# Attention on one core: one row-score pair at every key step, and the narrow sixth pair of each half job moved between the second and third value products

## What is computed

```python
def gqa_block_attention(q, k, v):           # 16 query heads, 4 key/value heads, head width 64
    ...
    def one_block(q_blk):
        s = jnp.einsum('bqhgd,bkhd->bhgqk', q_blk, k, preferred_element_type=F32) * scale
        pr = jax.nn.softmax(s, axis=-1).astype(v.dtype)
        return jnp.einsum('bhgqk,bkhd->bqhgd', pr, v)
```

## Time and profile before

| what | value |
|---|---|
| median of 3 runs | 3097.41 us (3095.95 to 3100.65) |
| span of the profiled execution | 3093.3 us |
| difference of the two (launch and end, outside the span) | 4.1 us |
| PE busy | 94% of the span |
| row scores ahead of job 0 | 807.9 to 831.58 us |
| jobs 0 to 13 and first half of job 14, with row scores | 831.58 to 1289.20 us |
| rest of the attention, without row scores | 1289.20 to 1336.40 us |
| one job in the steady part | 31.36 us |

### The profile page before, as it was taken

How to read it: one execution, slowest core, us unless ns; L and a number is a source line. 1 busy time by engine, 2 the same in 40 slices (tenths; PEclk the granted TensorE clock), 3 DMA queues, 4 the chain that set the end, 5 groups by cost and what they waited for, 6 DMA issues and landing times. The chain is left out here.

```text
span 3093.3 us, 28722 instructions
## 1 busy us (share of the span) xinstructions
PE 2916.4 (94%) x10163; PEld 1457.1 (47%) x10163; DVE 1591.3 (51%) x2480; ACT 740.7 (24%) x1557; POOL 1076.2 (35%) x971
## 2 busy tenths in 40 slices
PE   7998999999899999999969994988999999999999
PEld 4554554444455555444544442566444444444443
DVE  2433884345666666555654434446543444444446
ACT  2223755411133333300211115222030000000002
POOL 0002871000176767710022002832023445555442
PEclk9998999999899999999969996999999999999999
DMA  7001332100100000020178987003020111111101
GB/s 276 21 0 41 90 96 72 54 28 1 55 1 1 1 1 1 1 66 11 68 259 320 358 352 239 22 0 123 0 82 27 41 41 49 66 49 41 41 14 61
DMA packets 130686, 237.51 MB, mean 77 GB/s; under 512 B 25544, under 2 KB 81520, under 8 KB 120688
## 3 DMA queue, kind: packets, MB, share of 16 engines
q1 hardware_dynamic: 120016, 206.11, 18.8%
q0 software_dynamic: 5760, 16.78, 1.8%
q10 hardware_dynamic: 4768, 12.79, 1.1%
HBM read 235.65 MB, written 26.22 MB: 85 GB/s over the span
## 5 line engine op out<-in xcount | busy, mean ns | idle before, releaser
L3597 DVE TENSOR_TENSOR arena_d<-arena_d,ps 128x512 f32<-128x512 f32 x154 | 101.8, 684 | 389.2 <-PE ps L3472 389.2
L1366 DVE TENSOR_REDUCE arena_b<-ps 128x1 f32<-128x512 f32 (+1 forms) x384 | 217.3, 599 | 146.5 <-PE ps L1254 146.0
L3437 POOL TENSOR_TENSOR arena_b<-arena_b,arena_d 128x512 f32<-128x512 f32 x120 | 150.8, 1271 | 362.7 <-DVE arena_d L3619 361.3
L1348 POOL TENSOR_TENSOR arena_b<-arena_b 128x512 f32<-128x512 f32 x182 | 224.6, 1268 | 94.5 <-ACT arena_b L1330 94.5
L1254 PE MATMUL ps<-arena_d,arena_a 64*128 64x512 f32 (+1 forms) x768 | 237.1, 541 | 3.6 <-DVE arena_b L1357 2.9
L1273 PE MATMUL ps<-arena_a,arena_d 64*128 64x512 f32 x640 | 220.0, 607 | 2.4 <-ACT arena_b L1330 1.8
L3616 DVE TENSOR_TENSOR arena_b<-arena_b,ps 128x512 f32<-128x512 f32 x240 | 159.0, 685 | 32.7 <-POOL arena_b L3437 23.7
L1077 PE MATMUL ps<-ring,arena_b 128*128 128x512 f32 x384 | 167.4, 592 | 0.0
L564 PE MATMUL ps<-arena_b,ring 128*128 128x512 f32 x384 | 167.1, 593 | 0.0
L1330 ACT ACTIVATE arena_b<-ps 128x512 f32<-128x512 f32 x214 | 116.1, 595 | 212.8 <-PE ps L1279 212.8
L3472 PE MATMUL ps<-arena_a,ring 128*128 128x512 f32 x352 | 156.0, 602 | 3.0 <-DMA ring<-in_w_up 3.0
(11 more groups left out here) (614 smaller groups left out, 5492.3 us busy)
## 6 DMA issues: line engine op xcount, KB each, us to landing
ring<-in_w_gate SPq DMA_DIRECT2D x33, 1024.0 KB
ring<-in_w_up SPq DMA_DIRECT2D x33, 1024.0 KB
ring<-in_w_down SPq DMA_DIRECT2D x33, 1024.0 KB
ring<-in_w_in SPq DMA_DIRECT2D x10, 2048.0 KB, 9.8
ring<-in_w_mod SPq DMA_DIRECT2D x32, 512.0 KB, 3.8
yslots<-arena_a ACTq DMA_DIRECT2D x24, 512.0 KB, 4.5
arena_d<-in_w_gate SPq DMA_DIRECT2D x10, 1024.0 KB
arena_d<-in_w_up SPq DMA_DIRECT2D x10, 1024.0 KB
```

The costliest lines, as they stand in the source:

```text
L1348: eng.tensor_tensor(acc, first, prT[n % NPR], ALU.add).then_inc(s_pa, 1)
L1366: eng.tensor_reduce(mx3[j % 2][:, t, e, piece:piece + 1], ps[:, shared("s", u), 0:k1 - k0], AX.X, ALU.max).then_inc(s_mx, 1)
L3437: eng.tensor_tensor(o, o, dsum[0 if a == "a12" else 1], ALU.add).then_inc(s_comb, 1)
```

## The change

One row-score pair now stands at each key step: 6, 7, 8, 9, 10 in steps 0 to 4, and 0, 1, 2, 3, 4 in steps 5 to 9. The sixth pair, the narrow 11 or 5, no longer has a step. PE makes it after two of the five value products (`PV_FIRST = 2`). The order in which the three shared banks are given out follows PE's order, so in step 9 the narrow pair now takes its banks after the turned shifts and the row sums. DVE's program is changed to the same order: in step 9 it takes the maxima of the narrow pair after the copy of the shifts and ahead of the reciprocal.

```diff
-        BESIDE = (((1, 6),), ((1, 7),), ((1, 8), (1, 9)), ((1, 10),), ((1, 11),),
-                  ((2, 0),), ((2, 1),), ((2, 2), (2, 3)), ((2, 4),), ((2, 5),))
+        BESIDE = tuple((a, p) for a, p0 in ((1, 6), (2, 0)) for p in range(p0, p0 + 5))
 
         GROUP = 5
+        BETWEEN = {GROUP - 1: (1, 11), NT - 1: (2, 5)}
+        PV_FIRST = 2
...
             for j in range(NJOB):
                 for kt in range(NT):
                     shifted(j, kt)
-                    for ahead, pair in BESIDE[kt]:
-                        if j + ahead < NJOB:
-                            scores(j + ahead, pair)
+                    ahead, pair = BESIDE[kt]
+                    if j + ahead < NJOB:
+                        scores(j + ahead, pair)
                     if kt == NT - 1 and j + 1 < NJOB:
                         turn_shifts(j + 1)
                     if kt == NT - 1 and j >= 1:
                         row_sums(j - 1)
-                    if kt % GROUP == GROUP - 1:
-                        for i in range(kt + 1 - GROUP, kt + 1):
-                            pv(j, i)
+                    if kt in BETWEEN:
+                        for i in range(GROUP):
+                            if i == PV_FIRST:
+                                ahead, pair = BETWEEN[kt]
+                                if j + ahead < NJOB:
+                                    scores(j + ahead, pair)
+                            pv(j, kt + 1 - GROUP + i)
...
                 for kt in range(NT):
-                    for ahead, pair in BESIDE[kt]:
+                    ahead, pair = BESIDE[kt]
+                    if j + ahead < NJOB:
+                        largest(j + ahead, pair)
+                    if kt == NT - 1 and j + 1 < NJOB:
+                        shifts(j + 1)
+                    if kt in BETWEEN:
+                        ahead, pair = BETWEEN[kt]
                         if j + ahead < NJOB:
                             largest(j + ahead, pair)
                     if kt == GROUP - 1 and j + 1 < NJOB:
                         split(j + 1)
-                    if kt == NT - 1 and j + 1 < NJOB:
-                        shifts(j + 1)
                     if kt == NT - 1 and j >= 1:
                         scale(j - 1)
```

More of the change, by code:

```diff
@@ L1228, in build @@
             for kt in range(NT):
-                for ahead, pair in BESIDE[kt]:
-                    if j + ahead < NJOB:
-                        takes_pair(j + ahead, pair)
+                ahead, pair = BESIDE[kt]
+                if j + ahead < NJOB:
+                    takes_pair(j + ahead, pair)
                 if kt == NT - 1 and j + 1 < NJOB:
```

## The result

| | median | lowest to highest | runs |
|---|---|---|---|
| before | 3095.80 us | 3089.69 to 3100.65 | 12 |
| after | 3104.86 us | 3096.59 to 3108.19 | 12 |

A forecast was written before the change was run, and what follows sets the result against it. PE was taken as the bound, by how densely it streams. Net changeover cost of 2.6 us and 7.0 for the reciprocal sum to 9.6, making the median 3107.0 us from 3097.41, slower by 0.31%; range 3098.5 to 3112.

The forecast's parts named there:

- The double step: Third step of a half job, with two row-score pairs: weights wait for maxima, one array half lags; costs 0.78 us.
- The 9.70 of the prediction: Summed lengths of a half job's products in us, set against the 10.65 it takes, so about 0.95 is lost.
- the three places: Where a half job loses time: entry 0.10, third step 0.78, exit 0.10, together 0.98 us.
- The lag behind a lone narrow pair: Step after the third: e = 1 waits for its exponential, 0.52 us with late weights, leaving a gain of 0.26.
- Changing over: Narrow pair inside the value products: two more changes between 128-row and 64-row products cost 0.35 us a half job.
- Net +0.09 a half job: Cost 0.35 of the moved narrow pair less the 0.26 gained by spreading; x 29 = +2.6 us.
- The reciprocal: First row scores of jobs 2 to 14 wait for it behind the narrow maxima: 0.54 us, 13 times, +7.0 us.
- The offset: Profiled span 3093.3 lies 4.1 us under the median of the runs, 3097.41; the same was added to the forecast span.
- A: Rival at the next job's first row scores: the reciprocal is in time, only 2.6 us stays, 3100.0; chance 0.13.
- B: Rival at the step after the lone narrow pair: no lag, whole 0.78 gained, 3091.9 us, faster; chance 0.09.
- D: Rival at the value products: switching between 128-row and 64-row products costs nothing, 3096.8 us, no change; chance 0.04.
- C: Rival on DVE: one more long operation makes `split` end 0.3 late, 5 to 18 us more, 3112 to 3125; chance 0.07.

The follow-up runs named there:

- Experiment 5: Kernel before, with pairs dealt narrow, four full, narrow, the first ahead of the first step and one at each step: 3076.23 us, ratio 0.9940.
- experiment 4: Changed kernel with the four full pairs in steps one to four, narrow ones in the fifth step and the value products: 3088.84 us, ratio 0.9983.
- experiment 6: Kernel before, with a full pair ahead of the first step and a lone narrow pair at the second: 3088.24 us, ratio 0.9974 to the kernel before.
- Experiment 7: Changed kernel with full pairs first and DVE's reciprocal ahead of the narrow maxima: 3085.18 us, ratio 0.9972 to the kernel before.
- experiment 1: Changed kernel, but DVE takes the reciprocal and its multiplication ahead of the narrow pair's maxima: 3099.54 us, ratio 1.0016 to the kernel before.
- experiment 2: Changed kernel with the narrow pair after the first value product in place of the second: 3099.19 us, ratio 1.0015 to the kernel before.
- experiment 3: Changed kernel with the narrow pair after the third value product in place of the second: 3115.52 us, ratio 1.0068 to the kernel before.

## Why the prediction was right, step by step

**The losses of before.** The double step, 0.78 a half job, was read from rows alone. Experiment 5 shows it: with all six pairs in the half job and no double step it takes 9.95 for 10.65. These 0.70 are the 0.78 less the 0.09 of lag that every full step leaves, and that the longer lag of the double step had covered. The 9.70 of the prediction is a sum of rounded lengths; with 0.859 for a pair and 0.216 for a bf16 pair, the products of a half job stream for 9.67, and the three places, 0.98, then make up the whole 10.65.

**The lag behind a lone narrow pair.** Forecast: 10.65 - 0.43 - 0.26 = 9.96. Measured 9.95. Experiments 4 and 6 show the cause, once by taking the narrow pair from the third step and once by bringing a lone one back. The part that a mended order gets back is 0.43 and not the 0.52 of the prediction, because 0.09 of lag stands already behind every full step (the load at 1009.01 in the earlier trace rows, released by ACT, is such a one); the prediction's 0.52 was the whole, and the right number for its sum.

**Changing over.** Forecast 0.35 a half job. The value products with the pair take 5.23 for 4.44, that is 0.79, of which 0.43 is the pair: 0.36. Experiment 7 against 5 gives 0.35 again. Net +0.09 a half job and 2.6 us stand.

**The reciprocal.** The right mechanism, mis-sized: 0.54 a time was forecast, 0.37 measured, 4.8 us in place of 7.0. With T = 1022.37, the first transpose, the reciprocal ended at T + 7.90 (forecast T + 7.98), and the row scores were due at T + 7.69 (forecast T + 7.59), so the difference of the two long sums was 0.27 with the late load and not 0.44. The term that was mis-sized is the two narrow maxima. The prediction took 0.81 from the earlier trace rows and 0.03 behind them; from the start of the first (1026.25) to the start of the reciprocal (1026.92) it was 0.67. In the earlier trace rows the second maximum had waited for a lagging e = 1, and the recorded length of a maximum reaches beyond the start of the next operation: 1026.25 + 0.75 is 1027.00. All else in the two sums came 0.10 later than forecast on both sides. Experiments 1, 2 and 3 show that it is the reciprocal: it goes when DVE comes to it sooner by either way, and grows by 0.86 for 0.86.

**What was missing.** Transposes and row sums take 1.30 in place of 1.23, and the value products behind them 5.21 in place of 4.39 + 0.78 = 5.17. The fifth step now ends in a full pair, and the row sums take the bank of its e = 0. Their weights load at 1022.76, where 1022.70 would be the pace of before. Together 0.11 a job, 1.4 us over 13 jobs. The 0.07 is the wait of experiment 4 again, shorter. The maximum of e = 0 and the load of the row sums, in the changed kernel and then in experiment 4:

```profile
1021.96 0.69 DVE L1375 TENSOR_REDUCE arena_b<-ps 128x1 f32<-128x512 f32 x1 [0.65 <-PE ps L1259]
1022.76 0.23 PEld L1302 LDWEIGHTS ps<-arena_b,ones 128*64 128x64 f32 x4 [0.17 <-issue]
...
1012.24 0.42 DVE L1377 TENSOR_REDUCE arena_b<-ps 128x1 f32<-128x256 f32 x1 [0.22 <-PE ps L1260]
1012.78 0.23 PEld L1303 LDWEIGHTS ps<-arena_b,ones 128*64 128x64 f32 x4 [0.33 <-issue]
```

In both, the load comes 0.11 to 0.12 us after the end of the maximum, though one stands 0.39 behind the first transpose and the other 0.55. It is so in the steady jobs of all kernels but the kernel before and experiment 6, where the maximum is done 0.18 ahead and the load stands at 0.33. Why the value products behind them take 0.04 more, no row says.

The sum of what was measured is 29 x 0.09 + 13 x 0.37 + 1.4 = 8.8 us, against 8.9 in the attention of the trace and 8.7 by the ratio.

**The offset.** The prediction set the profiled span 4.1 us under the median. In every run of the changed kernel the time is 2.1 us over its span, so only 2.1 of the 4.1 is launch and end. The rest is that the execution profiled before was faster than the median of the three. As an offset added to before and after alike it changed nothing in the forecast difference; the median before came out at 3095.80 over twelve runs, 1.6 below the 3097.41 from which the forecast of 3107.0 was counted.

**The rivals.** A (the reciprocal in time) was close: 0.27 us decided it, and experiment 1 is that case, with 1.0016. B (no lag) and D (changing over is free) fell by the rows. C (`split` too late) did not come; it went the other way, below.

## What to carry to other kernels

When two halves of the array run beside each other, one late bank lets one half lag, and the lag (0.43 us in experiments 4 and 6) is paid at the next product that needs both. It shows in no idle time of PE, so count the streaming time of a stretch and compare. A short piece of work at a step gives the next step less time than product, exponential and weight load need behind each other (1.06 us here behind a full and behind a narrow pair alike), so short pieces belong last, or where nothing waits behind them. Spreading work evenly by number (one pair per step) isn't yet spreading it evenly by time, and a piece put into a gap elsewhere has its own price at both ends and its place in another engine's queue.

## What the runs showed of the hardware that was not expected

`split` became shorter, without any edit to it. In the earlier trace rows it takes 3.30 us from 1003.12. Two of its six operations, on 8 elements a partition, take 1.23 and 1.18 us; here they are, with two of POOL's additions from POOL's timeline:

```profile
1003.33 1.23 DVE L1376 CAST arena_b<-arena_b 128x8 bf16<-128x8 f32 x1
1004.59 1.18 DVE L1377 TENSOR_TENSOR arena_b<-arena_b 128x8 f32<-128x8 f32 x1
...
1003.23 1.29 POOL L1348 TENSOR_TENSOR arena_b<-arena_b 128x512 f32<-128x512 f32 x1
1004.45 1.29 POOL L1348 TENSOR_TENSOR arena_b<-arena_b 128x512 f32<-128x512 f32 x1
```

The cast ends at 1004.56, and the addition at 1004.52; the subtraction ends at 1005.77, and the next addition at 1005.74. In the changed kernel the timeline of DVE has

```profile
1010.58 0.18 DVE L1384 TENSOR_REDUCE arena_b<-arena_b 128x8 f32<-128x24 f32 x1
1010.79 0.32 DVE L1385 CAST arena_b<-arena_b 128x8 bf16<-128x8 f32 x1
1011.14 0.17 DVE L1386 TENSOR_TENSOR arena_b<-arena_b 128x8 f32<-128x8 f32 x1
```

and all six in 1.38. `split` now comes at the end of a run of POOL's additions, whose row in POOL's timeline is

```profile
1007.36 3.71 POOL L1357 TENSOR_TENSOR arena_b<-arena_b 128x512 f32<-128x512 f32 x3
```

They end at 1011.07, and the first cast ends at 1011.11. Experiment 3 is the case with no addition beside `split`. The narrow pair comes later there, POOL's last addition has ended at 1013.06, and the same cast and the same subtraction are short:

```profile
1013.64 0.19 DVE L1385 CAST arena_b<-arena_b 128x8 bf16<-128x8 f32 x1
1013.86 0.17 DVE L1386 TENSOR_TENSOR arena_b<-arena_b 128x8 f32<-128x8 f32 x1
```

Counted over `split` in the attention's jobs of all nine traces, 196 of these casts and subtractions start while one of POOL's additions runs, and each ends 0.03 to 0.05 us after that addition. The other 479 start with POOL idle and take 0.17 to 0.19. The reduction at the head of `split` takes 0.18 either way. The Trainium skill, "SBUF — State Buffer", section Who interferes with whom, says that a cast in a two-port mode and an operation with two SBUF inputs contend with a GpSimd operation that is running, and that the one which came first holds the shared ports to its end while the other blocks. The rows agree; whether this cast is in such a mode, no run here shows.

So the fear of rival C was about a number that depends on where POOL stands: the same six operations take 1.25 us in experiment 3 and 4.22 in experiment 6, with three long ones among them, by the moment at which they come. In experiments 5 (3.97) and 6 that third long operation, which rival C feared, did occur and cost nothing, but there no narrow pair stands ahead of `split`. With one ahead of it, as in the changed kernel, this case was not met.
